# A two-layer conformer/retention backbone on one core: an opening by channel in four groups of two tiles, and weights stored unit by unit

## What is computed

```python
for i in range(2):
    mod_x = silu(c) @ ada_w[i] + ada_b[i]          # the same for ctx, from c_ctx
    s1, c1, g1, s2, c2, g2 = split(mod_x, 6)       # 1024 values each
    h = rmsnorm(x, norm1_g[i]) * (1 + c1) + s1
    if i == 0: y = conv_module(h)                  # h @ pw1_w -> value * sigmoid(gate) -> 31-tap conv -> LN -> pw2
    else:      y = retention_mixer(h, hc)
    x = x + g1 * y
    h = rmsnorm(x, norm2_g[i]) * (1 + c2) + s2
    x = x + g2 * conv_ffn(h)                       # 1024 -> 2 * 2816 -> 3-tap conv, gate -> 1024
return rmsnorm(x, final_g)
```

## Time and profile before

| | us |
|---|---|
| median of 3 runs (1670.49 to 1671.51) | 1671.19 |
| profiled execution: its time | 1671.56 |
| profiled execution: its span | 1669.7 |
| PE busy in the span | 1641.5 (98%) |
| DVE busy | 957.8 (57%) |
| ACT busy | 677.5 (41%) |
| POOL busy | 169.5 (10%) |

### The profile page before, as it was taken

One profiled execution on the slowest core, in us unless ns is written; L12 is line 12 of the kernel. 1 busy time (PEld: TensorE's weight loads), 2 busy tenths in 40 slices (PEclk: granted clock), 3 DMA queues, 4 the chain that ended last, 5 costly groups with the idle time before them and its releaser, 6 DMA issues.

```text
span 1669.7 us, 25567 instructions
## 1 busy us (share of the span) xinstructions
PE 1641.5 (98%) x10040; PEld 1435.3 (86%) x10040; DVE 957.8 (57%) x1511; ACT 677.5 (41%) x1019; POOL 169.5 (10%) x180
## 2 busy tenths in 40 slices
PE   6999989999999999999999999999999999999998
PEld 4777758998888888888899999999999888888888
DVE  6899987763424342334368665656566754543445
ACT  4656667642323222223245333424144543333333
POOL 2488851000000000000000000000000000000000
PEclk9999999999999999999999999999999999999999
DMA  9777742221221212121113221312122324233321
GB/s 338 253 252 251 252 160 95 76 75 48 67 76 55 70 56 71 55 71 55 59 51 92 64 70 39 83 51 63 58 64 76 99 79 124 87 104 89 100 88 51
DMA packets 238543, 165.65 MB, mean 99 GB/s; under 512 B 5288, under 2 KB 214040, under 8 KB 238456
## 3 DMA queue, kind: packets, MB, share of 16 engines
q1 hardware_dynamic: 234600, 150.43, 29.8%
q0 software_dynamic: 2992, 10.88, 2.0%
q10 hardware_dynamic: 864, 3.15, 0.5%
HBM read 162.34 MB, written 2.10 MB: 98 GB/s over the span
## 4 chain that ended last, share of the span: by engine, by line
PE 82%; DVE 14%; ACT 3%; issue 1%; DMA 0%; ACTq 0%; DVEq 0%
PE ps L702 81%; DVE ps L1895 3%; DVE ps L1912 3%; DVE w_lo L1691 2%; DVE rstd L1697 1%; DVE H_lo L1732 1%; PE ps L907 0%; DVE tmp L1720 0%; DVE ps L1910 0%; ACT sq L1279 0%; DVE sq L1720 0%; ACT tmp L1279 0%; DVE rstd L1708 0%; ACT H_hi L1270 0%; DVE ps L1892 0%
## 5 line engine op out<-in xcount | busy, mean ns | idle before, releaser
L702 PE MATMUL ps<-H_hi,w_hi 128*128 128x512 f32 (+1 forms) x1712 | 583.3, 341 | 8.3 <-DVE H_lo L1794 5.0
L702 PE MATMUL ps<-H_lo,w_hi 128*128 128x512 f32 (+1 forms) x1712 | 578.8, 338 | 0.0
L702 PE MATMUL ps<-H_hi,w_lo 128*128 128x512 f32 (+1 forms) x1712 | 578.1, 338 | 0.0
L702 PEld LDWEIGHTS ps<-H_hi,w_hi 128*128 128x128 f32 x1712 | 324.8, 190 | 62.2 <-issue 24.4
L702 PEld LDWEIGHTS ps<-H_hi,w_lo 128*128 128x128 f32 x1712 | 324.8, 190 | 35.0
L702 PEld LDWEIGHTS ps<-H_lo,w_hi 128*128 128x128 f32 x1712 | 325.0, 190 | 34.3
L1691 DVE TENSOR_TENSOR w_lo<-w_raw,w_hi 128x1024 fp32r<-128x1024 f32 x208 | 255.0, 1238 | 108.0 <-ACT w_hi L1232 75.1
L702 PE MATMUL ps<-mid_hi,w_hi 128*128 128x512 f32 (+1 forms) x592 | 199.5, 337 | 0.6
L702 PE MATMUL ps<-mid_lo,w_hi 128*128 128x512 f32 (+1 forms) x592 | 198.3, 335 | 0.0
L702 PE MATMUL ps<-mid_hi,w_lo 128*128 128x512 f32 (+1 forms) x592 | 198.1, 335 | 0.0
L2228 DVE SCALAR_TENSOR_TENSOR tmp<-ps,par,tmp 128x511 f32<-128x511 f32 x66 | 41.6, 657 | 231.3 <-ACT tmp L1576 155.0
(11 more groups left out here) (278 smaller groups left out, 2097.2 us busy)
## 6 DMA issues: line engine op xcount, KB each, us to landing
w_raw<-in_ffn_w_in SPq DMA_DIRECT2D x88, 512.0 KB, 3.8
ada<-in_ada_w SPq DMA_DIRECT2D x40, 1024.0 KB, 6.3
w_raw<-in_ret_w_in SPq DMA_DIRECT2D x40, 512.0 KB, 3.9
w_raw<-in_ffn_w_out SPq DMA_DIRECT2D x32, 512.0 KB, 4.4
w_raw<-in_conv_pw_w SPq DMA_DIRECT2D x22, 512.0 KB, 8.7
w_raw<-in_ffn_w_out SPq DMA_DIRECT2D x16, 384.0 KB, 3.5
ada<-in_ada_w POOLq DMA_DIRECT2D x4, 1024.0 KB, 13.5
w_raw<-in_ret_w_out SPq DMA_DIRECT2D x8, 512.0 KB, 4.2
```

The source lines that it names most:

```text
L702: return nc.tensor.matmul(o, a, b, start=first, stop=last, skip_group_check=True)
```

## The change

It replaces the opening and stores the inputs in another layout.

- On the host, before the launch, x and ctx are laid out channel-major (`x_cols`), all parameters as one array of 128 rows (`params`), `ada_w` as groups with 8 KB in a row for each half group (`ada_groups`), and all other weights as units with 4 KB (3 KB for the chunk of 6 tiles) in a row for each partition (`w_units`). Before, a unit came in pieces of 512 bytes and a group in pieces of 2 KB.
- The four first groups now hold the shift and the scale of two tiles each: group `m` serves tiles `2m` and `2m + 1` (`first_shift` finds the column). DVE's `first_modulation(m)` runs four times, on half as many columns.
- x goes straight to `X` in four loads on SP's queue. There are no token or parameter transposes and no bn_stats: ACT squares the 8 tiles (8 ACTIVATE of 768), DVE adds them (7 adds of 768), and PE sums over channels with six one-column matmuls.
- POOL's queue waits for the second quarter of x and loads unit 0 before group 1.
- PE's order of the opening is new, and with it ACT's and DVE's.

```diff
-FIRST_GROUPS = [0, 2, 1, 3]
+FIRST_GROUPS = 4
...
         def load_first(eng, m, half):
-            rows = slice(half * D // 2, (half + 1) * D // 2)
-            g = FIRST_GROUPS[m]
-            eng.dma_start(ada_first[m][half], ada_w[0][rows, g * GROUP * P:(g + 1) * GROUP * P]
-                          .rearrange("(k p) n -> p k n", p=P)).then_inc(ada_first_in[m], 16)
+            eng.dma_start(ada_first[m][half], ada_groups[m, half].rearrange("p (k n) -> p k n", n=GROUP * P)) \
...
+            for n in range(KT // 2):
+                sp.dma_start(X[:, 2 * n:2 * n + 2, :], x_cols[:, 2 * n:2 * n + 2, :]).then_inc(x_in[n], 16)
+            sp.dma_start(ident[:], eye).then_inc(eye_in, 16)
             for dst, src in ((rrow[:], rope_row), (rcol[:], rope_col), (tcol[:], token_cols),
...
+                if isinstance(unit, int):
+                    src = w_units[unit, :, 0:kt * P]
+                else:
+                    src = w_units[ds(unit, 1), :, 0:kt * P].rearrange("a p n -> p (a n)")
                 if not (isinstance(unit, int) and unit < RING):
                     sp.wait_ge(lo_ready, unit - (RING - 1))
-                k = src.shape[0] // P
-                sp.dma_start(w_raw[:, r, 0:k * P].rearrange("p (k n) -> p k n", n=P),
...
                 for half in range(2):
                     load_first(pool, m, half)
-            load_gate_or_value(0)
+                load_gate_or_value(m)
             for half in range(2):
                 load_first(pool, 2, half)
...
+            pe.wait_ge(filled, 1)
+            pe.wait_ge(silu_c_ready, 2)
+            ada_products(0)
+            pe.wait_ge(x_added, KT - 1)
+            for t in range(6):
+                m = mm(tok_sums[:, t:t + 1], x_squares[:, t * P:(t + 1) * P], mean_of[:, 0:1], True, True)
+            m.then_inc(x_summed, 1)
...
-                pe.wait_ge(slot_read[p], S_PW1 // 2)
-            first_block(0, 0, 1)
+            first_block(0, 0, 2)
+            ada_products(1)
+            ada_transposes(1)
+            first_block(1, 0, 2)
             ada_products(2)
-            first_block(0, 1, 3)
             ada_transposes(2)
-            first_block(0, 3, 4)
-            pe.wait_ge(par_ready, 2)
+            first_block(0, 2, 4)
+            first_block(1, 2, 4)
             ada_products(3)
-            first_block(1, 0, 1)
             ada_transposes(3)
-            first_block(1, 1, 4)
-            first_block(0, KT // 2, KT - 2)
+            first_block(0, 4, 6)
+            first_block(1, 4, 6)
+            first_block(0, 6, KT)
             ada_products(4)
-            first_block(0, KT - 2, KT)
-            first_block(1, KT // 2, KT)
+            first_block(1, 6, KT)
             ada_transposes(4)
...
+            act.wait_ge(par_in, 16)
+            for v in range(2):
+                A(silu_c[:, :, v], par[:, C_COL + 8 * v:C_COL + 8 * v + 8], ACT.Silu).then_inc(silu_c_ready, 1)
+            for k in range(KT):
+                act.wait_ge(x_in[k // 2], 16)
+                if k >= 4:
+                    act.wait_ge(x_added, max(k - 4, 1))
+                A(norm_buf[k % 4], X[:, k, :], ACT.Square).then_inc(x_squared, 1)
+            A(tok_std_row, eps[:, 0:1], ACT.Sqrt)
             ada_copy(0)
-            ada_copy(1)
-            split_hi(0, 0)
+            act.wait_ge(x_summed, 1)
+            A(tok_rstd[:], tok_sums, ACT.Sqrt, bias=eps[:, 0:1]).then_inc(tok_std, 1)
...
+            for m in range(FIRST_GROUPS):
+                if m:
+                    ada_copy(m)
+                if m < 2:
+                    split_hi(m, m)
+                for j in (2 * m, 2 * m + 1):
+                    first_hi(j)
+            split_hi(2, 2)
+            split_hi(3, 3)
             ada_copy(4)
...
+                v.tensor_tensor(x_squares, norm_buf[0] if k == 1 else x_squares, norm_buf[k % 4], ALU.add) \
+                    .then_inc(x_added, 1)
+            dve.wait_ge(par_in, 16)
             dve.wait_ge(tok_std, 1)
             v.reciprocal(tok_rstd[:], tok_rstd[:]).then_inc(tok_rstd_ready, 1)
             dve.wait_ge(tok_rstd_ready, 1)
...
+            ada_sum(0, 0, 0)
+            first_modulation(0)
...
-            first_shifted(0)
-            split_lo(0, 0)
-            first_lo(0)
-            first_tiles(range(1, KT // 2))
-            split_lo(1, 1)
-            normed_rows(range(KT // 2, KT))
-            ada_sum(2, 0, FIRST_GROUPS[2])
-            ada_sum(3, 0, FIRST_GROUPS[3])
-            first_modulation(4, 1)
-            first_tiles(range(KT // 2, KT))
+            for m in range(FIRST_GROUPS):
+                normed_rows([2 * m, 2 * m + 1])
+                if m:
+                    ada_sum(m, 0, m)
+                    first_modulation(m)
+                if m < 2:
+                    first_shifted(2 * m)
+                    split_lo(m, m)
+                    first_lo(2 * m)
+                    first_tiles([2 * m + 1])
+                else:
+                    first_tiles([2 * m, 2 * m + 1])
             split_lo(2, 2)
...
+    w = np.asarray(inputs["ada_w"])
+    first = w[0][:, 0:2 * D].reshape(D, 2, FIRST_GROUPS, 2 * P).transpose(0, 2, 1, 3).reshape(D, 2 * D)
+    both = np.concatenate([first, w[0][:, 2 * D:], w[1]], axis=1)
+    groups = np.ascontiguousarray(both.reshape(2, KT // 2, P, 24, GROUP * P).transpose(3, 0, 2, 1, 4)
+                                  .reshape(24, 2, P, KT // 2 * GROUP * P))
...
+        k = w.shape[0] // P
+        units[unit, :, 0:k * P] = w[:, col:col + P].reshape(k, P, P).transpose(1, 0, 2).reshape(P, k * P)
```

More of the change, by code:

```diff
@@ L538, in load_pairs @@
-            def load_pairs(first, w, half, n):
-                def body(i):
-                    for q in range(2):
-                        for h in range(2):
-                            load(2 * first + 4 * i + 2 * q + h, 2 * q + h,
-                                 w[:, ds(i * (2 * P) + (q * P + h * half), P)])
-                with sp.Fori(0, n // 2) as i:
-                    body(i)
-            def load_cols(first, w, n):
-                with sp.Fori(0, n // 2) as i:
+                sp.dma_start(w_raw[:, r, 0:kt * P], src).then_inc(raw_ready[r], 16)
@@ L591, in _ @@
                         load_group(m)
[L592 to L599 removed]
+            load_ffn(FFN0)
+            load_range(2 * RET, 2 * (FFN1 - RET))
+            load_ffn(FFN1)
             for j in range(0, KT, 2):
@@ L877, in ada_products @@
                     pe.wait_ge(ada_row_ready, m)
-                first = isinstance(m, int) and m < 4
+                first = isinstance(m, int) and m < FIRST_GROUPS
                 for half in range(2):
@@ L2458, in shape_constants, with weight_units, put @@
     }
+def weight_units(inputs):
+    import numpy as np
+    pw1, pw2 = (np.asarray(inputs[n])[0] for n in ("conv_pw1_w", "conv_pw2_w"))
+    ret_in, ret_out = (np.asarray(inputs[n])[0] for n in ("ret_w_in", "ret_w_out"))
+    units = np.zeros((UNITS, P, KT * P), np.float32)
+    def put(unit, w, col):
+        k = w.shape[0] // P
+        units[unit, :, 0:k * P] = w[:, col:col + P].reshape(k, P, P).transpose(1, 0, 2).reshape(P, k * P)
+    for b in range(KT):
+        for h in range(2):
+            put(2 * (PW1 + b) + h, pw1, (1 - h) * D + b * P)
+        put(2 * PW2 + b, pw2, b * P)
+        put(2 * RET_OUT + b, ret_out, b * P)
+    for h in range(HEADS):
+        for part in range(5):
+            for u in range(2):
+                put(2 * (RET + 5 * h + part) + u, ret_in, part * D + h * DH + u * P)
+    for layer, first in enumerate((FFN0, FFN1)):
+        w_in, w_out = (np.asarray(inputs[n])[layer] for n in ("ffn_w_in", "ffn_w_out"))
+        f = 0
+        for n in CHUNKS:
+            for a in range(n):
+                for h in range(2):
+                    put(2 * (first + a) + h, w_in, h * F + (f + a) * P)
+            for b in range(KT):
+                put(2 * (first + n) + b, w_out[f * P:(f + n) * P], b * P)
+            first, f = first + n + 4, f + n
+    return units
 def kernel(**inputs):
@@ L2468 @@
     arrays, args = {}, []
-    for name, a in [(n, _np.ascontiguousarray(inputs[n])) for n in _INS] + list(shape_constants().items()):
+    for name, a in laid_out(inputs) + [("w_units", weight_units(inputs))] + [(n, _np.ascontiguousarray(inputs[n])) for n in _PLAIN] + list(shape_constants().items()):
         arrays[f"in_{name}"] = a
```

240 lines of the change are left out of this document (65 added, 175 removed).

## The result

The changed kernel took 1688.45 us (median of 4 runs, 1685.74 to 1689.62), the kernel before 1671.32 beside it: a ratio of 1.010 [1.0087, 1.0112], **17.1 us slower**. The sign was forecast with 0.84, the size was not: 8.3 us were expected, and 1688.45 lies 5.5 us outside the range. The profiled execution took 1688.82 us with a span of 1687.0, 17.3 us more than the span before.

What follows compares the result with a forecast made beforehand. Everything behind 59.4 us was taken to hang on DVE's list; ten steps put the opening's end at 68.1, less 0.4 for the method's excess: 8.3 us later, 1679.5 us on the median, range 1673.5 to 1683.

Steps and rivals of the forecast that it cites:

- slow clock: PE at half clock on group 0's products and the first pieces of units 0 and 1: 4.0 us, counted in full.
- step 1: PE's products of group 0 start at 17.6 us, when it lands, and take 3.6 us: end at 21.2.
- Base: Everything behind 59.4 us hangs on DVE's list; a microsecond won or lost before it is one in the total.
- the sign of being right: Among the signs: DVE's second both-phases sum comes 22 us behind the first.
- Step 2: PE's six token sums, root, reciprocal, diagonals and spread of 1/rms (1.53 us): ends at 25.9 us, before 24.1.
- Step 3: DVE's normed rows, shifted, `w_lo` and `H_lo` for the first tiles: 6.5 us, ending at 32.4.
- Steps 4 and 5: Rest of unit 0's piece 2.3 us, to 34.7; group 1's round trip, then `w_lo` of unit 1, to 40.7.
- Steps 6 to 8: Unit 1's piece 3.6 us, to 44.3; group 2 and two pieces, to 51.7; group 3 and three, to 61.1.
- Steps 9 and 10: Group 4, ACT's copy, sigmoid table and two sigmoids 5.0 us, to 66.1; DVE's L1997 and L2000 2.0, to 68.1.
- third rival: Loads late behind the opening: group 5 issued only after group 4's products, 1 to 2 us more, 1681.5; chance 0.12.
- first rival: Opening bound by its loads: group 3's products at 39.1 us, end 3.9 us earlier, 1667.3; chance 0.10.
- second rival: Layout relieves DVE (1676.0) or the clock falls less (1675.6), both 1672.1: slower by less; chance 0.17.

Runs made afterwards that it cites:

- the run with PE kept busy: Changed kernel plus matmuls that compute nothing on PE wherever it is idle in the opening: 1683.19 us, ratio 1.0067 to the kernel before.
- the run that is in order: Changed kernel with token sums first, each group's products and row one group ahead, groups 4 and 5 loaded a step earlier, early sigmoid table: 1670.56 us, ratio 0.9996.
- group 4 last: Changed kernel with group 4's products behind unit 1's last piece and ACT's copy of its row behind the first two sigmoids: 1691.70 us, ratio 1.0119.

## Why the prediction was wrong

The sign and the mechanism held, the size did not. Two terms of the sum failed. The slow clock was left out of the spread of 1/rms and of group 1's products (1.53 and 1.92 us in the sum, 2.87 and 2.57 measured). The late load of group 5, which the sum has at nothing, cost 4.7 us. Besides, group 0 landed 1.4 us later than step 1 has it. By the steps of the prediction, with what the profile shows at each:

- **Base.** "Everything behind 59.4 us hangs on DVE's list" held to 1.5 us: from the last both-phases sum to the end it was 1455.1 us before, 1453.6 to 1455.9 in 16 of 18 profiles, and 1457.1 in the two where PE waited over 3.5 us there. What I missed is that block 0, ahead of all that, isn't of fixed length: it took 26.5 us between the two sums, where the forecast named 22 as the sign of being right.
- **Step 1**, group 0: landed at 19.03, not 17.6. The DMA engines moved 341 GB/s from 6 to 14 us, not the 388 of before, and PE's 3.6 us of slow products measured 3.64. 1.4 us late.
- **Step 2**: the spread was taken from the earlier trace rows at 1.53 us, full clock, right behind a step that I had at half. It took 2.87; the granted clock was 0.54 from 26 to 29 us. With hand-overs, the rows were ready at 29.1, not 25.9: 3.2 late by here.
- **Step 3**: 6.5 us forecast, 6.4 measured.
- **Steps 4 and 5**: the piece ended 38.55 (0.6 more than forecast), group 1's products ran at 2.57 us, not 1.92, for I had let the clock recover over a piece of 4.5 us which ran at 0.50 throughout. PE had the `w_lo` of unit 1 at 45.30, 4.6 late.
- **Steps 6 to 8**: 2.9, 8.3 and 9.5 us against 3.6, 7.4 and 9.4. The clock fell once more (0.73 from 48 to 52 us). 5.0 late.
- **Steps 9 and 10**: 5.0 and 1.6, against 5.0 and 2.0. L1894 waited 4.21 us for ACT's sigmoids, as forecast.

The first sum was forecast 8.3 us later and came 13.2 later: 4.9 us. Steps 1, 2, 4 and 5 give 4.6 of them, steps 6 to 8 give 0.4, and step 10 takes 0.4 off: 72.69 us against the 68.1 of the sum. The rest is the 0.4 that the forecast took off because the same way of adding had come out that much long on the old order. (The profiled execution is 17.3 slower, so 9.0 us are missing there: these 4.9, the 4.7 below, less the 0.6 behind the last block.) The slow clock, "an unknown price" of 4.0, is at least 4.4 at the first sum and 5.3 in the total by the run with PE kept busy: the right kind of cost, but not counted at each of PE's steps behind a wait. The 0.6 us that came back at the end are luck: PE's ten matmuls on both phases took 3.46 us there and 4.95 in the kernel before.

- The other **4.7 us** are the third rival, "loads late behind the opening", which had "1 to 2 us more". Its mechanism was right to the word, its size was not worked out: a load of 5 us on top of PE's idle time ahead of it, two halves, each waited for (1.51 and 2.19 us), the second then multiplied at half clock (1.94 us against 1.06), with a unit's turn in block 0 behind both, and DVE on the value behind that. It should have been in the sum, since nothing in the list of the change could hide it.
- "If PE did reach its groups early, the loads would be next" holds in the run that is in order, and the first rival's sign with it: group 3 at 37.56 (39.1 forecast). Its arithmetic failed. The first sum followed 20.6 us behind group 3, not 16.4, since DVE's list, busy for all but 4.3 of 29.9 us, is then as long as PE's; so it came 1.3 us earlier than before, not 3.9.
- The second rival, the layout relieving DVE, fell with 20.5 against 20.6 us. The Trainium skill, "SBUF — State Buffer", section "SBUF: two separate sides", has DMA and engines on separate sides of SBUF; the runs agree that the pieces' size changed nothing for DVE.

In short: two tiles for each group could let work start early, but the change wrote each group's round trip over three engines in line with the pieces. The work it removed lay under the loads, the waits it added lay on DVE's path, and idle stretches of PE were mostly paid twice, once in waiting and once in clock.

## What to carry to other kernels

When work is cut into smaller steps that pass through several engines, issue each step's first stage one step ahead; the same parts in that order, with the token sums first and two loads issued a step earlier, gave back 17.9 us. Cost every instruction behind a wait of PE at both clocks, also the small ones, and ask of each load what its issue hangs on after the reordering. A faster layout shows only where someone waits for the load: the same edit was worth nothing in one order and, as far as the intervals tell, 1.6 us in another.

## What the hardware showed that was not expected

- Matmuls that compute nothing, in waits that are there anyway, gave 5.3 us of 1688, and nothing where a load was the floor.
- The granted clock in the records isn't the whole of it: it stands at 1.00 from 19 to 23 us in the changed kernel, while the products of group 0 took 3.64 us there and 1.92 behind PE's idle matmuls. Columns: as above.

```profile
19.00:23.00 4.00, 3.97 (x19) 1.08 (x19) 0.00 (x0) 0.27 (x1) 0.53 (x2) 1.00 1.02 429
```

- How long PE waited doesn't tell alone whether the clock falls. The four sums over `conv` and the ten matmuls on both phases at the end of the convolution stage take 1.56 and 3.46 us at full clock, and did so behind waits of 1.76 to 1.85 us (six kernels), 2.06 (the layout alone), 2.37 and 2.60. Behind 1.88 (group 4 last) and 2.03 us (the kernel before) the ten took 4.99 and 4.95. Behind 2.22 and 2.59 us the four took 2.93 and 2.79 and the ten 3.71 and 3.96, and behind 3.60 and 3.67 the ten took 5.07 and 5.09. The kernels with 2.59 and 2.60 us differ only in the opening; here are both, in this order:

```profile
213.37 2.79 PE L655 MATMUL ps<-conv,mean_of 128*128 128x512 f32 x4 [2.59 <-DVE sq L1900]
215.96 3.96 PE L655 MATMUL ps<-both_phases,conv 128*128 128x392 f32 x10
```
```profile
213.54 1.56 PE L655 MATMUL ps<-conv,mean_of 128*128 128x512 f32 x4 [2.60 <-DVE sq L1907]
214.93 3.46 PE L655 MATMUL ps<-both_phases,conv 128*128 128x392 f32 x10
```

- Halves of a group in 8 KB rows moved at 424 GB/s from 14 to 28 us, where the kernel before had 363 in 2 KB pieces, and the changed kernel in the old pieces 365. The kernel before with the new layout had 406.
